# Gated attention on one core: each decay level forms only its own score blocks, ScalarE places the coarse ones, and the fine ones take one masked copy of the diagonal blocks

## The chip, the cores and the metric

The kernel runs on one core of one Trainium2 chip. The metric is the device time of one execution in microseconds (us). The whole of a hybrid encoder block is computed in one launch: an input projection, a gated linear attention and a convolution side by side, an output projection, a cross attention and a mixture of experts. The change lies in the gated linear attention.

## What is computed

Only the attention part is shown. Queries and keys have 64 channels per head, values 128; there are 4 heads, 1024 positions, and a decay per channel and position in each of the two directions.

```python
GLA_HEADS = 4; GLA_DV = 128; GLA_DK = 64; CHUNK = 64
def gla_direction(q, k, v, log_a, strict):
    # o_i = sum_{j<=i (or j<i if strict)} q_i diag(prod_{m=j+1..i} a_m) k_j^T v_j
    bcum = jnp.cumsum(log_a..., axis=-2)
    diff = bcum[..., :, None, :] - bcum[..., None, :, :]
    decay = jnp.exp(jnp.where(mask[:, :, None], diff, -jnp.inf))
    scores = jnp.einsum('bhnid,bhnjd,bhnijd->bhnij', qc, kc, decay)
    o_intra = jnp.einsum('bhnij,bhnjv->bhniv', scores, vc)
    ...
o = rms_norm(o_f + o_b, norm_g)          # forward plus backward direction
return (o * silu(r)).astype(q.dtype)
```

## The kernel before

The instructions of each engine are written out in the order in which they run, one block of code per engine, with semaphores between them; nothing is moved by a scheduler. Only the loop over experts at the end is a hardware loop.

The attention works on windows of 128 positions, 8 of them (`TT`), and on two pairs of heads, `p` = 0 and 1. Within a window the scores of both directions form one 128x128 matrix per head. A product of two decays can't be formed for all pairs of positions from one common reference without overflow, so the matrix is put together from levels. Level 0 is the diagonal (no decay at all). Level l = 1 to 7 takes the pairs of positions whose halves of a block of 2s positions differ, with s = 64, 32, 16, 8, 4, 2, 1 (`LEVELS`): each gets a reference at the middle of its own block. Before the change each level forms the full 128x128 product of every window, and a mask picks the entries that belong to it.

For each `p` the engines run this loop:

- VectorE (DVE), step l: multiplies keys and queries with the decays (`KQ` or `KQ2`, L1242 and L1243, 128x1024 each), computes the exponents of the next level into `EX` (`exponents`, L1209 to L1212, four of 128x512), and then `select(l)`: four instructions that move the products of level l from PSUM into `Ssc`, one bank of four windows each. For l = 0 that is a plain copy (L1225), for the others a copy under a mask (L1227).
- ScalarE (ACT): the exponential of `EX` for each level, one instruction of 128x2048 (L729). After that of level 0 it also drains four products of the memory projection (`drain_memory`, L608).
- TensorE (PE), level l (L1843): 16 matmuls, one per window and head of the pair. Keys of 64 channels are the stationary operand, 128 queries move. Levels alternate between banks 0 to 3 and 4 to 7 of PSUM. The trace shows two matmul records and two weight loads for each of these f32 matmuls, so 32 records a level. Behind level 0 stand two chunks of the memory projection (`memory_chunk`, L1788), 64 records of 256 moving columns, and a wait until ScalarE has drained them, since level 1 takes over their banks.

PE's level l+1 needs DVE's step l (`s_kq`); DVE's `select(l)` needs PE's level l (`s_gram`); PE's level l needs `select(l-2)` to be done with the banks. Behind the loop PE turns the decayed keys (L1855), forms the window updates (L1865), and then the outputs from `Ssc` and the states (L1877 to L1879).

## Time and profile before

| | us |
|---|---|
| median of 3 runs | 2769.03 |
| lowest, highest | 2765.13, 2769.28 |
| the profiled execution | 2766.17 |
| its span in the trace | 2764.4 |
| level loop, p = 0: first KQ to last select | 361.9 to 417.2 |
| level loop, p = 1: memory products 493.1 to 507.1, last select ends | 557.5 |

The profiled execution's own time is 1.8 us longer than the span of its trace. The page gives PE 91% busy, DVE 68%, ScalarE 47%. The expert loop takes the last 1,660 us and most of PE's time; the two level loops take about 55 and 65 us of the span. The granted clock of TensorE has two levels, 2.4 GHz (shown as 1.00) and 1.2 GHz (0.50). A "record" is a line of the trace for one pass of a matmul; its duration holds a latency that overlaps with its neighbours, so prices here are taken from the distance between starts.

### The profile page before, as it was taken

What the parts mean: (1) busy time and instruction counts of PE and PEld (TensorE: products, weight loads), DVE (VectorE), ACT (ScalarE), POOL (GpSimd) and SP (SyncE); (2) the same over time, 40 slices, a digit from 0 to 9 for tenths busy, and PEclk for the clock granted to TensorE, in tenths of its full rate; (3) what the DMA queues carried; (4) which work ended last, traced back from release to release, by engine and by line L of the source; (5) the groups of instructions that cost most, each with busy time, mean ns of one, the idle gap of its engine ahead of it and who ended that gap; (6) DMA issues with size and microseconds to landing.
All of it is one profiled execution on the core that took longest, in us unless ns stands there. A gap on an engine that the chain in (4) does not pass through costs nothing.

```text
span 2764.4 us, 36052 instructions
## 1 busy us (share of the span) xinstructions
PE 2521.2 (91%) x12280; PEld 2064.2 (75%) x12281; DVE 1872.7 (68%) x1955; ACT 1287.3 (47%) x1374; POOL 384.7 (14%) x321
## 2 busy tenths in 40 slices
PE   4999888879897898599999999999999999999994
PEld 3889686859784697477777777777777777777773
DVE  4399693851404325687887787768877778888776
ACT  4211433230314223366665565556555566676554
POOL 0000000001000005211211211122211122121111
PEclk9999865769899995799999999999999999999997
DMA  3111200211010023998997888779878788999776
GB/s 117 51 57 47 76 31 0 77 61 39 31 46 16 1 98 100 312 313 292 340 351 257 274 284 269 256 217 336 280 251 283 261 282 286 339 364 324 245 248 246
DMA packets 268690, 536.19 MB, mean 194 GB/s; under 512 B 11100, under 2 KB 45200, under 8 KB 268528
## 3 DMA queue, kind: packets, MB, share of 16 engines
q1 hardware_dynamic: 249952, 474.51, 48.6%
q0 software_dynamic: 16384, 57.68, 9.0%
q10 hardware_dynamic: 2288, 3.08, 0.4%
q8 instruction: 47, 0.77, 0.1%
q14 instruction: 19, 0.16, 0.0%
HBM read 491.45 MB, written 43.78 MB: 194 GB/s over the span
## 4 chain that ended last, share of the span: by engine, by line
PE 77%; DVE 13%; issue 4%; ACT 4%; DMA 1%; DVEq 1%; ACTq 0%; POOL 0%; POOLq 0%
PE PS L2082 11%; PE PS L2084 11%; PE PS L2083 11%; PE PS L1748 9%; PE PS L2090 6%; PE PS L2087 6%; PE PS L1905 3%; PE PS L1971 3%; DVE wlo L1543 2%; PE PS L2052 1%; PE PS L1958 1%; DVE Ssc L1227 1%; PE PS L1923 1%; PE PS L1925 1%; PE PS L1788 1%
## 5 line engine op out<-in xcount | busy, mean ns | idle before, releaser
L1543 DVE TENSOR_TENSOR wlo<-raw,whi 128x2048 fp32r<-128x2048 f32 x395 | 897.9, 2287 | 202.4 <-ACT whi L864 181.9
L864 ACT CAST whi<-raw 128x2048 fp32r<-128x2048 f32 x395 | 746.0, 1911 | 199.1 <-PE PS L2090 137.6
L2082 PE MATMUL PS<-whi,xhi 128*128 128x512 f32 x1056 | 439.1, 416 | 0.5 <-DVE wlo L1543 0.5
L2084 PE MATMUL PS<-whi,xlo 128*128 128x512 f32 x1056 | 414.0, 392 | 0.0
L2083 PE MATMUL PS<-wlo,xhi 128*128 128x512 f32 x1056 | 412.4, 391 | 0.0
L2084 PEld LDWEIGHTS PS<-whi,xlo 128*128 128x128 f32 x1056 | 198.9, 188 | 43.7
L2082 PEld LDWEIGHTS PS<-whi,xhi 128*128 128x128 f32 x1056 | 200.4, 190 | 39.8 <-DVE wlo L1543 5.2
L2083 PEld LDWEIGHTS PS<-wlo,xhi 128*128 128x128 f32 x1056 | 199.5, 189 | 40.0
L2082 PE MATMUL PS<-whi,hhi 128*128 128x512 f32 x512 | 202.6, 396 | 0.0
L2084 PE MATMUL PS<-whi,hlo 128*128 128x512 f32 x512 | 199.7, 390 | 0.0
L2083 PE MATMUL PS<-wlo,hhi 128*128 128x512 f32 x512 | 199.4, 389 | 0.0
L2090 PE MATMUL PS<-wlo,xtl 128*128 128x512 f32 x480 | 193.5, 403 | 0.0
L2087 PE MATMUL PS<-whi,xtl 128*128 128x512 f32 x480 | 187.5, 391 | 0.0
L507 POOL COPY idxc<-TG 128x2 uint32 (+1 forms) x35 | 23.7, 678 | 917.8 <-PE PS L2052 515.9
L1132 DVE SCALAR_TENSOR_TENSOR yT<-u_pad,CWT,yT 128x1024 f32<-128x1024 f32 x120 | 144.2, 1275 | 0.0
L528 POOL DMA_INDIRECT acc_scratch<-yb,idxs x66 | 135.1, 2047 | 22.0 <-issue 22.0
L513 POOL DMA_INDIRECT xs<-h_scratch,idxc x70 | 132.2, 1889 | 19.9 <-issue 17.7
L920 ACT ACTIVATE yb<-PS,row_gate 128x512 f32<-128x512 f32 x64 | 44.0, 687 | 189.1 <-PE PS L2090 127.0
L1314 DVE TENSOR_TENSOR xres<-xres,PS 128x256 f32<-128x256 f32 x64 | 26.9, 420 | 150.6 <-PE PS L1905 82.0
L2090 PEld LDWEIGHTS PS<-wlo,xtl 128*128 128x128 f32 x480 | 90.0, 188 | 30.4 <-issue 13.6
L2084 PEld LDWEIGHTS PS<-whi,hlo 128*128 128x128 f32 x512 | 96.1, 188 | 20.4
L2082 PEld LDWEIGHTS PS<-whi,hhi 128*128 128x128 f32 x512 | 96.1, 188 | 19.9
(376 smaller groups left out, 4757.7 us busy)
## 6 DMA issues: line engine op xcount, KB each, us to landing
raw<-in_exp_w_up SPq DMA_DIRECT2D x267, 1024.0 KB, 6.1
raw<-in_exp_w_down SPq DMA_DIRECT2D x128, 1024.0 KB, 6.8
ring<-in_w_in SPq DMA_DIRECT2D x11, 1024.0 KB, 5.3
xres<-in_x SPq DMA_DIRECT2D x4, 1024.0 KB, 12.9
ring<-in_xattn_wk SPq DMA_DIRECT2D x4, 1024.0 KB, 6.9
ring<-in_xattn_wv SPq DMA_DIRECT2D x4, 1024.0 KB, 4.9
ring<-in_w_out SPq DMA_DIRECT2D x4, 1024.0 KB, 5.0
xres<-in_x SPq DMA_DIRECT2D x1, 4096.0 KB, 13.4
```

The costliest lines, as they stand in the source:

```text
L513: nc.gpsimd.indirect_dma_start(xs[0:rows, b, :], None, h3_dram, bass.IndirectOffsetOnAxis(ap=idxc[0:rows, b:b + 1], axis=0)).then_inc(s_xs ...
L528: nc.gpsimd.indirect_dma_start(acc_dram, bass.IndirectOffsetOnAxis(ap=idxs[0:rows, b:b + 1], axis=0), yb[0:rows, b, :], None, compute_op=A ...
L864: nc.scalar.copy(whi[:, chunk_slot(c, NSPL), :], raw[chunk_slot(c, NRAW)][:]).then_inc(s_whi, 1)
L1132: ins = nc.vector.scalar_tensor_tensor(out=yT[:, c, :], in0=uc, scalar=w, in1=yT[:, c, :], op0=ALU.mult, op1=ALU.add)
L1543: nc.vector.tensor_tensor(wlo[:, chunk_slot(c, NSPL), :], raw[chunk_slot(c, NRAW)][:], whi[:, chunk_slot(c, NSPL), :].bitcast(F), ALU.subtract
L1748: ins = pe.matmul(out, lhs, rhs, start=(k == 0 and i == 0), stop=(k == KT - 1 and i == 2))
L1905: ins = pe.matmul(bank_groups(n, 256), a, b, start=(k == 0 and i == 0), stop=(k == KT - 1 and i == 2))
L2082: pe.matmul(o, hi[:, k, :], wh, start=first and bias is None, stop=False)
L2083: pe.matmul(o, hi[:, k, :], wl, start=False, stop=False)
L2084: ins = pe.matmul(o, lo[:, k, :], wh, start=False, stop=stop and kk == 3)
L2087: pe.matmul(ot, both_parts, wh, start=first, stop=False)
L2090: ins = pe.matmul(ot, both_parts, wl, start=False, stop=stop and kk == 3)
```

## The change

Level 1 forms only the 64x64 blocks off the diagonal of each window, level 2 only the 32x32 blocks next to the diagonal ones within each half, and level 0 and levels 3 to 7 only the 32x32 blocks on the diagonal. `gram_banks` puts a level into two banks (0 and 1, or 2 and 3), one per head of the pair, so that the memory projection keeps banks 4 to 7 for itself. ScalarE copies level 1 and level 2 into `Ssc` (4 copies each). `select` runs for level 0 and levels 3 to 7 alone, with one instruction over a new tile `Dsc` of 128x512, and at the end ScalarE copies `Dsc` into the diagonal blocks of `Ssc` (4 copies). The exponential is issued in two halves, keys and queries. The last two memory chunks of each `p` are cut into four halves, one behind each of levels 1 to 4. The masks shrink from seven of 128x128 to five of 128x32.

```diff
+        DIAG = (0, 3, 4, 5, 6, 7)
+        def gram_banks(L):
+            return 2 * (L % 2)
+        def diag_scores(L, rows=slice(0, P)):
+            b = gram_banks(L)
+            return PS[rows, b:b + 2, 0:256].rearrange("p h (w c) -> p h w c", w=TT)
...
                 for l in range(8):
-                    act.wait_ge(s_sub, 8 * p + l + 1)
-                    nc.scalar.activation(EX[:], EX[:], ACT.Exp, scale=1.0 / TAU).then_inc(s_ex, 1)
-                    if l == 0:
-                        drain_memory(range(8 * p + 4, 8 * p + 8))
+                    for i in range(2):
+                        act.wait_ge(s_sub, 16 * p + 2 * l + i + 1)
+                        nc.scalar.activation(EX[:, i, :], EX[:, i, :], ACT.Exp, scale=1.0 / TAU).then_inc(s_ex, 1)
+                    if l == 2:
+                        act.wait_ge(s_gram, 2 * (8 * p + 2))
+                        for hh in range(2):
+                            for h in range(2):
+                                rows, cols = slice(64 * h, 64 * (h + 1)), slice(64 * (1 - h), 64 * (2 - h))
+                                ins = nc.scalar.copy(Ssc[rows, hh, :, cols], PS[rows, gram_banks(1) + hh, :].rearrange(
+                                    "p (w c) -> p w c", w=TT))
+                        ins.then_inc(s_plc, 1)
+                    if l == 3:
+                        act.wait_ge(s_gram, 2 * (8 * p + 3))
+                        for q in range(4):
+                            rows, other = slice(32 * q, 32 * (q + 1)), q ^ 1
+                            ins = nc.scalar.copy(scores(rows, slice(32 * other, 32 * (other + 1))), diag_scores(2, rows))
+                        ins.then_inc(s_plc, 1)
+                    if 3 <= l < 7:
+                        drain_memory((8 * p + l + 1,))
...
+                act.wait_ge(s_sel, 6 * (p + 1))
+                for q in range(4):
+                    rows = slice(32 * q, 32 * (q + 1))
+                    ins = nc.scalar.copy(scores(rows, rows), Dsc[rows, :, :, :])
+                ins.then_inc(s_plc, 1)
                 act.wait_ge(s_U, 14 * (p + 1))
...
                 def select(l):
-                    for b in range(4):
-                        hh, half = b // 2, b % 2
-                        L = 8 * p + l
-                        dve.wait_ge(s_gram, 4 * L + b + 1)
...
-                            ins = nc.vector.copy_predicated(
-                                scores, masks[:, l - 1:l, :].broadcast_to([P, 4, P]), products)
-                        ins.then_inc(s_sel, 1)
+                    L = 8 * p + l
+                    dve.wait_ge(s_gram, 2 * (L + 1))
+                    if l == 0:
+                        if p:
+                            dve.wait_ge(s_plc, 3 * p)
+                        ins = nc.vector.tensor_copy(Dsc[:], diag_scores(L))
+                    else:
+                        dve.wait_ge(s_sel, 6 * p + DIAG.index(l))
+                        mask = masks[:, l - 3:l - 2, :].unsqueeze(1).broadcast_to([P, 2, TT, 32])
+                        ins = nc.vector.copy_predicated(Dsc[:], mask, diag_scores(L))
+                    ins.then_inc(s_sel, 1)
...
                         pe.wait_ge(s_kq, 9 * p + l)
-                        if l >= 2:
-                            pe.wait_ge(s_sel, 4 * (L - 1))
+                        if l in (3, 4):
+                            pe.wait_ge(s_plc, 3 * p + l - 2)
+                        elif l >= 2:
+                            pe.wait_ge(s_sel, 6 * p + DIAG.index(l - 2) + 1)
...
+                    size = 64 if l == 1 else 32
+                    for w in range(TT):
+                        for q in range(P // size):
+                            partner = q ^ 1 if l in (1, 2) else q
+                            for hh in range(2):
+                                hp = slice(GDK * hh, GDK * (hh + 1))
+                                keys = slice(P * w + size * q, P * w + size * (q + 1))
+                                queries = slice(P * w + size * partner, P * w + size * (partner + 1))
+                                ins = pe.matmul(PS[size * q:size * (q + 1), gram_banks(L) + hh, size * w:size * (w + 1)],
+                                                K_[hp, keys], Q_[hp, queries], start=True, stop=True)
+                                if w == TT - 1 and q == P // size - 1:
+                                    ins.then_inc(s_gram, 1)
+                    if 1 <= l < 5:
+                        memory_chunk(4 * p + 2 + (l - 1) // 2, ((l - 1) % 2,))
                 pe.wait_ge(s_kq, 9 * p + 8)
-                pe.wait_ge(s_sel, 32 * (p + 1))
+                pe.wait_ge(s_sel, 6 * (p + 1))
```

How the instructions of the loop stand on three engines, for p = 0. PE, before: `x16` is one level of 16 matmuls, `mT,ring` the memory projection (an f32 matmul has two records in the trace), and the row with `ident` is the turning of the keys behind the loop.

```order
L1788 MATMUL PS<-mT,ring 128x256 x32
L1843 MATMUL PS<-qT,kT 128x128 x16
L1788 MATMUL PS<-mT,ring 128x256 x32
L1843 MATMUL PS<-KQ 128x128 x16
L1843 MATMUL PS<-KQ_60 128x128 x16
L1843 MATMUL PS<-KQ 128x128 x16
L1843 MATMUL PS<-KQ_60 128x128 x16
L1843 MATMUL PS<-KQ 128x128 x16
L1843 MATMUL PS<-KQ_60 128x128 x16
L1843 MATMUL PS<-KQ 128x128 x16
L1855 MATMUL PS<-ident,KQ_60 128x128 x16
```

PE, at the same place after the change:

```order
L1822 MATMUL PS<-mT,ring 128x256 x32
L1883 MATMUL PS<-qT,kT 32x32 x64
L1883 MATMUL PS<-KQ 64x64 x32
L1822 MATMUL PS<-mT,ring 128x256 x8
L1883 MATMUL PS<-KQ_60 32x32 x64
L1822 MATMUL PS<-mT,ring 128x256 x8
L1883 MATMUL PS<-KQ 32x32 x64
L1822 MATMUL PS<-mT,ring 128x256 x8
L1883 MATMUL PS<-KQ_60 32x32 x64
L1822 MATMUL PS<-mT,ring 128x256 x8
L1883 MATMUL PS<-KQ 32x32 x64
L1883 MATMUL PS<-KQ_60 32x32 x64
```

The 32 memory matmuls behind level 0 are now four groups of 8 behind levels 1 to 4, and a level has 64 matmuls of 32x32 (32 of 64x64 at level 1) in place of 16.

DVE, before, from the step of level 1 to that of level 3 (the copies into `Ssc` are `select`):

```order
L1242 TENSOR_TENSOR KQ_60<-EX,kT 128x1024
L1243 TENSOR_TENSOR KQ_60<-EX,qT 128x1024
L1209 TENSOR_TENSOR EX<-Bf 128x32x16
L1210 TENSOR_TENSOR EX<-Rb 128x32x16
L1211 TENSOR_TENSOR EX<-Rb 128x32x16
L1212 TENSOR_TENSOR EX<-Bf 128x32x16
L1227 COPY_PREDICATED Ssc<-masks,PS 128x512 x4
L1242 TENSOR_TENSOR KQ<-EX,kT 128x1024
```

DVE after the change, from the exponents that step 3 computes:

```order
L1243 TENSOR_TENSOR EX<-Bf 128x128x4
L1244 TENSOR_TENSOR EX<-Rb 128x128x4
L1245 TENSOR_TENSOR EX<-Rb 128x128x4
L1246 TENSOR_TENSOR EX<-Bf 128x128x4
L1259 COPY_PREDICATED Dsc<-masks,PS 128x512
L1273 TENSOR_TENSOR KQ<-EX,kT 128x1024
```

The four masked copies of a level are one, and steps 1 and 2 have none at all.

ScalarE after the change, from the exponentials of level 0 on (before, this was one exponential of 128x2048, four drains of `kx` and seven more exponentials):

```order
L741 ACTIVATE EX<-EX 128x1024 x6
L747 COPY Ssc<-PS 64x8x64 x4
L741 ACTIVATE EX<-EX 128x1024 x2
L754 COPY Ssc<-PS 32x16x32 x4
L618 COPY kx<-PS 128x256
L741 ACTIVATE EX<-EX 128x1024 x2
L618 COPY kx<-PS 128x256
L741 ACTIVATE EX<-EX 128x1024 x2
L618 COPY kx<-PS 128x256
L741 ACTIVATE EX<-EX 128x1024 x2
L618 COPY kx<-PS 128x256
L741 ACTIVATE EX<-EX 128x1024 x2
```

The placements stand behind the exponentials of levels 2 and 3, and the drains, which stood together behind the first exponential, are spread over levels 3 to 6.

## Rows read from the trace of the kernel before

**Rows 1.** Page, part 4: the chain that ended last, by engine and line

```profile
PE 77%; DVE 13%; issue 4%; ACT 4%; DMA 1%; DVEq 1%; ACTq 0%; POOL 0%; POOLq 0%
```

**Rows 2.** Timeline of one level, p = 0: start us, us, engine, line, names, count, idle before

```profile
388.35 2.55 DVE L1227 COPY_PREDICATED Ssc<-masks,PS 128x512 f32<-128x512 uint8 x4
388.46 1.91 ACT L729 ACTIVATE EX<-EX 128x2048 f32<-128x2048 f32 x1 [5.33 <-DVE EX L1212]
390.80 1.21 DVE L1242 TENSOR_TENSOR KQ<-EX,kT 128x1024 f32<-128x1024 f32 x1
391.92 1.22 DVE L1243 TENSOR_TENSOR KQ<-EX,qT 128x1024 f32<-128x1024 f32 x1
393.17 0.69 DVE L1209 TENSOR_TENSOR EX<-Bf 128x512 f32<-128x512 f32 x1
393.19 6.21 PEld L1843 LDWEIGHTS PS<-KQ 64*128 64x128 f32 x32 [1.03 <-DVE KQ L1243]
393.19 6.50 PE L1843 MATMUL PS<-KQ 64*128 64x128 f32 x32 [0.73 <-DVE KQ L1243]
...
395.59 2.56 DVE L1227 COPY_PREDICATED Ssc<-masks,PS 128x512 f32<-128x512 uint8 x4
```

**Rows 3.** Timeline, p = 0: first step of the loop and its end

```profile
361.88 1.22 DVE L1242 TENSOR_TENSOR KQ<-EX,kT 128x1024 f32<-128x1024 f32 x1
...
364.35 5.87 PEld L1843 LDWEIGHTS PS<-KQ 64*128 64x128 f32 x32 [4.20 <-issue]
...
414.64 2.52 DVE L1227 COPY_PREDICATED Ssc<-masks,PS 128x512 f32<-128x512 uint8 x4
...
417.31 3.65 PE L1855 MATMUL PS<-ident,KQ 128*128 128x128 f32 x16 [3.13 <-DVE Ssc L1227]
418.44 0.58 ACT L735 COPY KEt<-PS 128x512 f32<-128x512 f32 x1 [6.47 <-PE PS L1855]
```

**Rows 4.** Timeline, p = 1: level 0, the memory products, levels 1 and 2, last select

```profile
489.62 3.31 PEld L1843 LDWEIGHTS PS<-qT,kT 64*128 64x128 f32 x32 [0.33 <-issue]
...
491.42 0.21 ACT L725 ACTIVATE TTd<-TTd 128x16 f32<-128x16 f32 x1
491.49 0.68 DVE L1211 TENSOR_TENSOR EX<-Rb 128x512 f32<-128x512 f32 x1
492.09 0.68 DVE L1212 TENSOR_TENSOR EX<-Bf 128x512 f32<-128x512 f32 x1
...
493.05 13.68 PEld L1788 LDWEIGHTS PS<-ring,mT 128*128 128x128 f32 x64
...
507.17 0.37 ACT L608 COPY vx<-PS 128x256 f32<-128x256 f32 x1 [3.08 <-PE PS L1788]
507.44 1.91 ACT L729 ACTIVATE EX<-EX 128x2048 f32<-128x2048 f32 x1
...
507.59 3.30 PEld L1843 LDWEIGHTS PS<-KQ 64*128 64x128 f32 x32 [0.86 <-ACT vx L608]
...
509.38 1.23 DVE L1242 TENSOR_TENSOR KQ<-EX,kT 128x1024 f32<-128x1024 f32 x1 [7.28 <-ACT EX L729]
...
554.96 2.52 DVE L1227 COPY_PREDICATED Ssc<-masks,PS 128x512 f32<-128x512 uint8 x4
```

**Rows 5.** Windows: us, busy of PE, PEld, DVE, ACT, POOL, then the granted clock

```profile
337.00:345.00 8.00, 5.19 (x32) 5.19 (x32) 3.06 (x6) 7.94 (x9) 0.00 (x0) 0.74 0.38 128
345.30:349.00 3.70, 3.70 (x13) 3.08 (x13) 3.67 (x8) 3.67 (x4) 0.00 (x0) 0.68 0.02 4
497.00:507.00 10.00, 10.00 (x47) 8.57 (x46) 5.07 (x9) 0.93 (x3) 0.00 (x0) 1.00 0.30 105
507.60:518.40 10.80, 6.99 (x64) 6.60 (x64) 8.98 (x12) 3.66 (x2) 0.00 (x0) 1.00 0.67 196
518.40:557.00 38.60, 32.53 (x160) 31.05 (x160) 38.43 (x53) 9.55 (x5) 0.00 (x0) 0.50 0.00 0
```

**Rows 6.** L1788 in 345 to 361 us: duration min/median/max ns, first and last start

```profile
L1788 PEld LDWEIGHTS PS<-mT,ring x64: 190/190/337, 345.3 to 360.0; 128*128 128x128 f32 x64
```

**Rows 7.** Timeline, PE: the matmuls with the fewest moving columns

```profile
1035.48 3.46 PE L1984 MATMUL PS<-rw,h3T 128*128 128x32 f32 x16
...
1077.90 0.37 PE L2010 MATMUL PS<-Mb,onesb 128*128 128x32 bf16 x8
...
1237.73 0.71 PE L2056 MATMUL PS<-ident,xs 64*128 64x64 f32 x8
```

**Rows 8.** Groups by line: mean ns, and the idle time of ScalarE before the state products end

```profile
L735 ACT COPY KEt<-PS 128x512 f32<-128x512 f32 x8 | 4.7, 585 | 14.6 <-PE PS L1855 14.6
L608 ACT COPY kx<-PS 128x256 f32<-128x256 f32 x8 | 2.5, 375 | 0.3 <-PE PS L1788 0.3
L737 ACT ACTIVATE EX<-Bf 128x1024 f32<-128x1024 f32 x2 | 2.1, 1056 | 19.7 <-PE PS L1865 19.7
```

**Rows 9.** Timeline of the kernel's start: the last mask, and TensorE's first wait

```profile
6.73 0.29 DVE L1024 SCALAR_TENSOR_TENSOR masks<-xor,mtmp 128x128 uint8<-128x128 int32 x1
7.61 1.06 ACT L589 ACTIVATE sig<-mem_tm 128x1024 f32<-128x1024 f32 x1
```

More of the change, by code:

```diff
@@ L134, in build @@
         before = sb("before", [P, P], F, 198)
-        masks = sb("masks", [P, 7, P], U8, 198.5)
+        masks = sb("masks", [P, 5, 32], U8, 198.5)
         W2 = sb("W2", [2 * RANK, 2, GK], F, 199.5)
@@ L142, in build @@
         smx = sb("smx", [P, 4, 4], F, 203.4375)
-        xor = sb("xor", [P, P], I32, 203.5)
-        mtmp = sb("mtmp", [P, P], F, 204)
+        xor = sb("xor", [P, 32], I32, 203.5)
+        mtmp = sb("mtmp", [P, 32], F, 204)
         PVr = sb("PVr", [64, P], F, 204.5)
@@ L721, in _ @@
                 drain_memory(range(8 * p, 8 * p + 4))
+                scores = lambda rows, cols: Ssc[rows, :, :, cols]
                 if p == 0:
@@ L740, in _ @@
                     act.wait_ge(s_lnv, 19)
+                    act.wait_ge(s_plc, 6)
                     split_y(1)
@@ L1019, in _ @@
             nc.vector.tensor_tensor(xor[:], xor[:], mtmp[:].bitcast(I32), ALU.bitwise_xor).then_inc(s_mask, 1)
-            for l, s in enumerate(LEVELS):
-                dve.wait_ge(s_mask, 2 * l + 1)
+            dve.wait_ge(s_mask, 1)
+            nc.vector.tensor_scalar(xor[:], xor[:], 31, None, ALU.bitwise_and).then_inc(s_mask, 1)
+            for l, s in enumerate(LEVELS[2:]):
+                dve.wait_ge(s_mask, 2 * l + 2)
                 nc.vector.tensor_scalar(mtmp[:], xor[:], float(2 * s), None, ALU.is_lt).then_inc(s_mask, 1)
-                dve.wait_ge(s_mask, 2 * l + 2)
+                dve.wait_ge(s_mask, 2 * l + 3)
                 nc.vector.scalar_tensor_tensor(out=masks[:, l, :], in0=xor[:], scalar=float(s), in1=mtmp[:],
@@ L1112, in _ @@
             w_in_lo(4)
-            dve.wait_ge(s_pad, 2 * CT)
+            dve.wait_ge(s_const, 7 + 2 * CT)
             cv = 0
@@ L1214, in select @@
                 def select(l):
-                    for b in range(4):
-                        hh, half = b // 2, b % 2
-                        L = 8 * p + l
-                        dve.wait_ge(s_gram, 4 * L + b + 1)
-                        if l and b == 0:
-                            dve.wait_ge(s_sel, 4 * L)
-                        scores = Ssc[:, hh, 4 * half:4 * half + 4, :]
-                        products = PS[:, 4 * (L % 2) + b, :].rearrange("p (w c) -> p w c", w=4)
-                        if l == 0:
-                            ins = nc.vector.tensor_copy(scores, products)
-                        else:
-                            ins = nc.vector.copy_predicated(
-                                scores, masks[:, l - 1:l, :].broadcast_to([P, 4, P]), products)
-                        ins.then_inc(s_sel, 1)
+                    L = 8 * p + l
[9 more added lines that the diff above has]
+                    ins.then_inc(s_sel, 1)
                 exponents(0)
@@ L1247, in _ @@
                     else:
-                        nc.vector.tensor_tensor(wins(EX[:, 0, :]), tot(0), wins(Bf[:]), ALU.subtract)
+                        nc.vector.tensor_tensor(wins(EX[:, 0, :]), tot(0), wins(Bf[:]), ALU.subtract
+                                                ).then_inc(s_sub, 1)
                         nc.vector.tensor_tensor(wins(EX[:, 1, :]), tot(1), wins(Rb[:]),
                                                 ALU.subtract).then_inc(s_sub, 1)
-                    select(l)
-                dve.wait_ge(s_ex, 9 * p + 8)
+                    if l in DIAG:
+                        select(l)
+                dve.wait_ge(s_ex, 17 * p + 16)
                 nc.vector.tensor_tensor(KQ2[:, 0, :], EX[:, 0, :], kT[:, p, :], ALU.mult)
@@ L1772, in _, with memory_chunk @@
             norm_turn("x", TT)
-            def memory_chunk(c):
+            def memory_chunk(c, halves=(0, 1)):
                 nonlocal g
                 pe.wait_ge(s_ring[slot_of[g]], 16 * fills[g])
-                for i in range(2):
+                for i in halves:
                     m = 2 * c + i
@@ L1789, in memory_chunk @@
                     ins.then_inc(s_mm["mem"], 1)
-                g += 1
+                if halves[-1] == 1:
+                    g += 1
             n = 0
@@ L1833, in _ @@
                         pe.wait_ge(s_kq, 9 * p + l)
-                        if l >= 2:
-                            pe.wait_ge(s_sel, 4 * (L - 1))
+                        if l in (3, 4):
+                            pe.wait_ge(s_plc, 3 * p + l - 2)
+                        elif l >= 2:
+                            pe.wait_ge(s_sel, 6 * p + DIAG.index(l - 2) + 1)
                     K_, Q_ = (kT[:, p, :], qT[:, p, :]) if l == 0 else (
                         (KQ, KQ2)[(l - 1) % 2][:, i, :] for i in range(2))
-                    for b in range(4):
-                        hh, half = b // 2, b % 2
-                        for w in range(4):
-                            a = slice(P * (4 * half + w), P * (4 * half + w + 1))
-                            hp = slice(GDK * hh, GDK * (hh + 1))
-                            ins = pe.matmul(PS[:, 4 * (L % 2) + b, P * w:P * (w + 1)], K_[hp, a], Q_[hp, a],
-                                            start=True, stop=True)
-                        ins.then_inc(s_gram, 1)
```

26 lines of the change are left out of this document (13 added, 13 removed).

## The prediction

> **What bounds the kernel now.** I read the chain that ended last first: it is PE for 77%, DVE for 13% [rows 1], and most of PE's part is the expert loop, which the change doesn't touch. So the question is what the two level loops cost, and I read them in the timeline, one level at a time. A level of p = 0 repeats every 7.24 us (388.35 to 395.59). DVE never pauses in it: 2.4 us for the two products KQ (390.80 to 393.17), 2.4 us for four exponents, 2.5 us for the four masked copies. PE's 32 records take 6.2 us of it and PE then waits 0.73 us for DVE; ScalarE waits 5.33 us [rows 2]. So DVE sets the loop, but PE is only 0.7 us behind it. In p = 1 something else comes first: 64 records of the memory projection run from 493.05 to 507, ScalarE's drains stand ahead of the exponential, and DVE idles 7.28 us until 509.38 [rows 4]. The ends of the loops are the last select, 414.64 + 2.52 = 417.2 and 554.96 + 2.52 = 557.5, for which the turning of the keys waits [rows 3, 4]. Whatever is saved before these two points shortens the kernel one for one, since all that follows hangs on them.
>
> **DVE's part.** One masked copy of 128x512 costs a quarter of the 2.5 us, 0.62 us: the new select has the same 128x512 elements. So a step falls from 7.24 to 7.24 - 1.85 = 5.4 us, and steps 1 and 2, without a select, to 4.8 us. If nothing else held it, DVE would come out 6 x 1.85 + 2 x 2.47 = 16 us earlier in p = 0, and by more in p = 1, where it waits now. The new form of the instruction reads two banks in place of one; no row shows that, and I take the price per element as unchanged.
>
> **ScalarE's part.** Two exponentials of 128x1024 cost 2 x 1.06 = 2.1 us where one of 128x2048 cost 1.91 [rows 2, 8]; the first half starts while DVE is still at the second, so the result is not later. The placements are 4 copies with 512 elements a partition, at 0.585 us each 2.3 us [rows 8], at levels 2 and 3. With a drain of 0.37 us the fullest step has 2.1 + 2.3 + 0.4 = 4.8 us, below every cycle found here; cover is the 5.33 us that ScalarE idles. Two new waits stand ahead of work on ScalarE: for PE's level 1 and level 2. Behind them are the exponentials of levels 3 and 4, which need DVE's exponents, and these come later than those products in the schedule below. PE's levels 3 and 4 wait for the placements; they too come later by 5 us and more. The last four copies (2.3 us) fall into the 9.9 us in each p in which ScalarE waits for the state products [rows 8]. If that cover were gone they would cost 2.3 us per p. The masks at the start end at 7.0 us, before ScalarE has even begun the first norm's sums [rows 9]: nothing.
>
> **PE's part, on which all hangs.** A level has 128 records of 32 columns in place of 32 records of 128, so as many weight columns as before. What is a short record's price? A record of 128 columns costs (3.30 - 0.19) / 31 = 100 ns at the full clock [rows 4] and (6.21 - 0.33) / 31 = 190 ns at half [rows 2]. The router's matmuls, which move only 32 columns against 128 columns of weights, cost (3.46 - 0.39) / 15 = 205 ns at half clock [rows 7]. So the weight columns set the price, not the moving ones, and a quarter of the columns would be 25 and 48 ns. The shortest spacing in the trace is (0.37 - 0.19) / 7 = 26 ns, at half clock, bf16 with 32 moving columns [rows 7], each with its own weight load; I take no record under 27 ns. Bounds: 27 ns at best, the 190 or 100 ns of today's record at worst. I take 27 ns at the full clock and 48 ns at half, since the same f32 operand, 64 rows high, is nearest. A level then costs 128 x 27 = 3.5 us at the full clock, 6.1 us at half; level 1, 64 records of 64 columns, 3.2 or 6.1 us. One thing could make it cheaper: neighbouring matmuls now alternate between the two halves of the array's rows. The Trainium skill (TensorE: Matmul & The Clock Gate, Part 3) says that matmuls on different row groups run at the same time; no row of this trace has two short ones side by side, and by it the half-clock levels would take 3.5 us and the sum below would gain another 13 us.
>
> A memory half is 16 records. Warm that is 16 x (13.68 - 0.19) / 63 = 3.4 us [rows 4]. From a cold start the 64 records of p = 0 took 14.7 us from first to last start against 13.5, 1.3 us more [rows 6], so 4.7 us.
>
> **The clock.** It stands at 1.00 through the memory products, stays there through two levels (507.6 to 518.4) and is 0.50 for the rest of the loop, though PE is busy 32.5 of 38.6 us in it [rows 5]. It fell within 337 to 345 after a pause and was back within 4 us of the memory products' start. So I take it as 1.00 from level 2 until level 5 (a memory half every 7 us), as 0.50 at levels 6 and 7, and at level 1 as 0.50 in p = 0 (20 us of pause before it) and 1.00 in p = 1.
>
> **The sum.** With these prices PE is the slower one, since its level and a memory half, 6.9 us, exceed DVE's 5.4. p = 0: level 1 starts at 364.3 as now. + 6.1 (level 1) + 4.7 (half) = 375.1; + 3 x (3.5 + 3.4) for levels 2 to 4 = 395.8; + 3.5 (level 5) + 6.1 + 6.1 = 411.5; + 0.8 for the hand-over and the last select = 412.3, against 417.2: -4.9 us. p = 1: the first exponential's query half can follow DVE's exponents (492.8) at 493.9, KQ is done at 495.2, and nothing waits for the memory products any more. 495.2 + 3.2 + 3.4 = 501.8; + 20.7 = 522.5; + 3.5 + 12.2 = 538.2; + 0.8 = 539.0, against 557.5: -18.5 us. Together -23.4 us. The profiled execution took 2766.17 us, so 2742.8; the median of the runs is 2.9 us above that execution, within their own spread of 4 us, so a median could come out at 2743 to 2746. I say 2743.
>
> **Both bounds of the same case.** With 27 ns everywhere DVE sets the second half of the loop: the same working gives 404.0 and 533.7, together -37, 2729. With 40 ns at the full clock levels 2 to 5 take 5.1 us each, -10 us, 2756.
>
> **Rival 1, a short record has a price of its own.** The kernel turns 64-row tiles with 64 moving columns at (0.71 - 0.22) / 7 = 70 ns each at the full clock [rows 7], more than half the price of its double. If 70 ns is what any short f32 record costs, a level is 9.0 us at either clock. p = 0 ends at 440, p = 1 at 571: +36, 2803. It decides from 49 ns on, where both loops sum to what they take now; 60 ns gives +19, 2785. Against it stands the 26 ns row, for it the fact that those are bf16. The Trainium skill (the same page, Part 1) names such a price, about 62 ns for every matmul when the hardware's decoder is off; the 26 ns row says that it is on here, and 62 ns would give 2789. This rival is the slower one; 0.22.
>
> **Rival 2, the clock doesn't hold.** Short matmuls on a quarter of the columns are light work, and 32 records of 128 columns already let the clock fall. If each memory half starts cold (4.7 to 4.9 us) and each level costs 48 ns, the loops end at 427 and 555, together +8, 2774. With the clock low all the way and 6.8 us for each half (16 x 427 ns, twice the warm spacing), +27, 2793. For it: the 0.50 at 518.4 to 557 [rows 5]. Against it: two whole levels without any memory product kept 1.00. 0.12.
>
> **Rival 3, the memory halves eat the gain of p = 0.** They run in PE's idle time now (345 to 360 [rows 6], while DVE prepares the decays) and stand between the levels afterwards. With short records at 45 to 49 ns and a clock that holds, p = 0 loses 5 us and p = 1 gains 5 to 9: 2761 to 2766. 0.08.
>
> **How the numbers follow.** Forecast 0.58 (2729 to 2757), rival 1 0.22 (2772 to 2803 and beyond), rival 2 0.12 (2768 to 2793), rival 3 0.08. The range goes from 2729 to 2793: it leaves out the upper end of rival 1, some 0.11, and 0.04 below. A measurement tells 0.2% from no change, 5.5 us. Faster by more: the forecast, half of rival 3 and a little of the rest, 0.64. Within: the other half of rival 3 and the low end of rival 2, 0.10. Slower: 0.26.
>
> **What would show it.** In the trace of the changed kernel: PE's matmuls of a level, first to last start, 3.5 us at clock 1.00 and 6.1 at 0.50; the granted clock near 1.00 from 376 to 399 and from 489 to 526; memory halves of 3.4 us; one masked copy of 0.7 us a level; DVE idle before it, released by PE, not by ScalarE; the last select at 412 and, counted from the start of level 0 in p = 1 (489.6 before), 49.4 us later. It would be wrong with a spacing over 49 ns, with the clock at 0.50 between the halves, or with DVE waiting for the placements on ScalarE.

## The result, and the profile after

The changed kernel takes 2730.85 us (median of 4 runs, 2719.98 to 2739.17); runs of the kernel before beside it have a median of 2769.16, 38 us more. The ratio on record is 0.9848, 95% interval 0.9829 to 0.9868, which is 42 us of the kernel before (37 to 47). A second timing of the same kernel gave 2731.03 and 0.9864 (0.9848 to 0.9881), 38 us. So the gain is 38 to 42 us, where 2743, 23 us, was forecast. That lies at the fast end of the forecast's range of 2729 to 2793: the median is 2 us inside it, and the ratio, taken of the 2769.03 of before, gives 2727, 2 us outside. The profiled execution took 2719.98 us, its span is 2718.2.

The chain that ended last, as page part 4 gives it for the changed kernel, reads as before [rows 1] but for one point of DVE:

```profile
PE 77%; DVE 12%; issue 4%; ACT 4%; DMA 2%; DVEq 1%; ACTq 0%; POOL 0%; POOLq 0%; SPq 0%
```

One level of p = 0 in the timeline of the changed kernel, the same place as [rows 2]: start us, us, engine, line, names, count, idle before.

```profile
388.15 1.21 DVE L1273 TENSOR_TENSOR KQ<-EX,kT 128x1024 f32<-128x1024 f32 x1
389.28 1.22 DVE L1275 TENSOR_TENSOR KQ<-EX,qT 128x1024 f32<-128x1024 f32 x1
390.53 0.69 DVE L1243 TENSOR_TENSOR EX<-Bf 128x512 f32<-128x512 f32 x1
390.55 1.56 PE L1883 MATMUL PS<-KQ 64*32 64x32 f32 x128 [3.33 <-DVE KQ L1275]
...
391.86 1.06 ACT L741 ACTIVATE EX<-EX 128x1024 f32<-128x1024 f32 x1 [2.89 <-DVE EX L1244]
...
392.94 0.72 DVE L1259 COPY_PREDICATED Dsc<-masks,PS 128x512 f32<-128x512 uint8 x1
...
393.56 1.22 DVE L1273 TENSOR_TENSOR KQ<-EX,kT 128x1024 f32<-128x1024 f32 x1
```

A level takes 393.56 - 388.15 = 5.41 us, where it took 7.24. DVE has no pause in it. PE's 128 short records take 1.56 us in all, 32 records of 128 columns took 6.50, and PE now waits 3.33 us for DVE. PE, which had 0.7 us to spare beside DVE, no longer sets anything here.

The levels behind which a memory half stands, and the ends of the two loops (timeline, changed kernel; the first select is that of p = 0, the second that of p = 1):

```profile
364.56 1.99 PE L1883 MATMUL PS<-KQ 64*64 64x64 f32 x64 [23.14 <-DVE KQ L1275]
366.47 4.70 PE L1822 MATMUL PS<-mT,ring 128*128 128x256 f32 x16
371.10 1.29 PE L1883 MATMUL PS<-KQ 64*32 64x32 f32 x128
372.32 3.72 PE L1822 MATMUL PS<-mT,ring 128*128 128x256 f32 x16
...
401.70 0.71 DVE L1259 COPY_PREDICATED Dsc<-masks,PS 128x512 f32<-128x512 uint8 x1
...
478.17 1.23 DVE L1273 TENSOR_TENSOR KQ<-EX,kT 128x1024 f32<-128x1024 f32 x1 [1.05 <-ACT EX L741]
...
517.73 0.72 DVE L1259 COPY_PREDICATED Dsc<-masks,PS 128x512 f32<-128x512 uint8 x1
```

The loops end at 402.4 and 518.4 us, where they ended at 417.2 and 557.5 [rows 3, 4]: 14.8 us come from p = 0, another 24.3 from p = 1, 39 in all. DVE's wait of 7.28 us in p = 1 [rows 4] is gone, and the first KQ of p = 1, which waited 2.05 us for the exponential before, waits 1.05. The span is 46 us shorter; the other 7 lie behind the loops, where nothing was changed. The stretch from the last output of the attention to the end took between 2151 and 2166 us in the traces of this case (2157 before, 2151 in this one), so the total of a single run can't be read closer than that. The loops are read in the traces, and the sum in several runs.

ScalarE's placements in the same trace: two groups between the exponentials, and one behind the loop, with 6.67 us of idle time after it out of the 9.9 us of before [rows 8]. DVE, which sets the loop, doesn't wait for them, so they cost nothing.

```profile
376.15 2.26 ACT L741 ACTIVATE EX<-EX 128x1024 f32<-128x1024 f32 x2 [0.37 <-DVE EX L1244]
378.43 2.34 ACT L754 COPY Ssc<-PS 32x512 f32<-32x512 f32 x4
...
406.69 2.49 ACT L765 COPY Ssc<-Dsc 32x512 f32<-32x512 f32 x4
...
415.85 1.06 ACT L768 ACTIVATE EX<-Bf 128x1024 f32<-128x1024 f32 x1 [6.67 <-PE PS L1905]
```

### The profile page after: what moved, and what is told of

Read it like the earlier page. It is cut to its first block, busy times and chain, and to the rows that moved or that the text cites. A ratio compares the mean times of both kernels' runs of the same rounds, so it can differ in the third digit from the quotient of the medians.

```text
span 2718.2 us, 38787 instructions
## 1 busy us (share of the span) xinstructions
PE 2442.7 (90%) x13622; PEld 1989.0 (73%) x13689; DVE 1840.1 (68%) x1900; ACT 1303.5 (48%) x1414; POOL 383.1 (14%) x321
## 4 chain that ended last, share of the span: by engine, by line
PE 77%; DVE 12%; issue 4%; ACT 4%; DMA 2%; DVEq 1%; ACTq 0%; POOL 0%; POOLq 0%; SPq 0%
PE PS L2123 12%; PE PS L2125 11%; PE PS L2124 11%; PE PS L1782 9%; PE PS L2131 6%; PE PS L2128 6%; PE PS L1946 3%; PE PS L2012 3%; DVE wlo L1577 1%; PE PS L2093 1%; PE PS L1999 1%; PE PS L1964 1%; PE PS L1966 1%; PE PS L1965 1%; ACT whi L896 1%
## 5 line engine op out<-in xcount | busy, mean ns | idle before, releaser
L2124 PE MATMUL PS<-wlo,xhi 128*128 128x512 f32 x1056 | 412.3, 390 | 0.0
L523 POOL DMA_INDIRECT xs<-h_scratch,idxc x70 | 128.1, 1830 | 20.0 <-issue 17.9
L938 ACT COPY low_up<-PS 64x512 f32<-64x512 f32 x60 | 35.0, 584 | 158.3 <-PE PS L2131 158.3
```

What stands on the lines that cost most here:

```text
L523: nc.gpsimd.indirect_dma_start(xs[0:rows, b, :], None, h3_dram, bass.IndirectOffsetOnAxis(ap=idxc[0:rows, b:b + 1], axis=0)).then_inc(s_xs ...
L2124: pe.matmul(o, hi[:, k, :], wl, start=False, stop=False)
```

## Experiments on the price of a short record

The forecast took 27 to 48 ns for a record; the trace has (1.29 - 0.19) / 127 = 8.7 ns, where 0.19 us is the duration of the last record itself (0.24 us at the lower clock). Neighbouring matmuls of the changed kernel lie on different tiles of the array: heads alternate between row halves, and the four blocks of a window between groups of 32 columns. Theory A is that tiles run side by side and the forecast's price holds for one tile. Theory B is that a short record is cheap by itself.

**same_tile**: consecutive matmuls stay on one tile; only their order differs.

```diff
-                    for w in range(TT):
-                        for q in range(P // size):
-                            partner = q ^ 1 if l in (1, 2) else q
-                            for hh in range(2):
+                    for q in range(P // size):
+                        partner = q ^ 1 if l in (1, 2) else q
+                        for hh in range(2):
+                            for w in range(TT):
```

> The changed kernel with the loops of a level turned round: for each block row and each head the 8 windows follow one another, so that 8 neighbouring matmuls (16 records) use the same 64 rows and the same 32 columns of the array. Theory A (short matmuls of different tiles run side by side, and that makes a record cost 9 ns): without neighbours in other tiles the record goes back to the 25 to 27 ns of the prediction at clock 1.00 and about 50 ns at 0.50; a level takes 3.4 us or 6 us and not 1.3. Theory B (a short weight load is simply cheap, and the tiles have nothing to do with it): 9 ns, a level of 1.3 us, as before the edit. By A the kernel takes 0 to 10 us more than the changed one, by B the same time.

It took 2750.73 us (one run). Timeline of its PE:

```profile
341.57 5.73 PE L1883 MATMUL PS<-qT,kT 64*32 64x32 f32 x128 [4.08 <-DVE EX L1210]
...
381.60 3.72 PE L1822 MATMUL PS<-mT,ring 128*128 128x256 f32 x16
385.25 3.54 PE L1883 MATMUL PS<-KQ 64*32 64x32 f32 x128
388.71 3.72 PE L1822 MATMUL PS<-mT,ring 128*128 128x256 f32 x16
...
412.63 3.65 PE L1895 MATMUL PS<-ident,KQ 128*128 128x128 f32 x16 [1.56 <-DVE KQ L1290]
...
490.49 5.99 PE L1883 MATMUL PS<-KQ 64*64 64x64 f32 x64 [2.04 <-DVE KQ L1275]
...
496.41 5.47 PE L1822 MATMUL PS<-ring,mT 128*128 128x256 f32 x16
501.80 3.54 PE L1883 MATMUL PS<-KQ 64*32 64x32 f32 x128
```

(3.54 - 0.19) / 127 = 26.4 ns a record, the forecast's 27. Level and memory half take 7.1 us, PE has no pause in these levels, and it leads. The granted clock is 0.98 from 376 to 399 us. So theory A holds: what the forecast priced is the record on one tile. At clock 0.50 it is 43 ns there, where 48 was forecast: (5.73 - 0.24) / 127 for the 128 records of level 0, which start at 341.57.

**same_tile_timed**: the same kernel, in rounds.

> The kernel same_tile once more, now timed in rounds beside the kernel before: the changed kernel with its short score matmuls in an order in which neighbours lie on the same tile of the array, all else as it is. Its trace showed a level of 128 short records at 3.54 us and loops that ended where the prediction had put them (412.6 and 543.7 us). By the shift of the loops against the kernel before, 575.0 - 21.7 or so, the difference should be 20 to 24 us, so 2745 to 2749 beside a kernel before of 2769; if what lies behind the loops hangs on how warm TensorE was left, up to 10 us either way.

2750.58 us (2743.4 to 2758.7), ratio 0.991 (0.9876 to 0.9945): 25 us faster than the kernel before (15 to 34). The changed kernel wasn't in these rounds. Against its own rounds same_tile is 20 us slower by the medians, 13 to 17 us by the ratios, and its two loops end 22 us later in the traces. The order of the matmuls alone decides about half of the gain: 22 of the 39 us in the loops.

**two_row_halves** (heads alternate, one column group after another) and **column_tiles** (one head after the other, the four column groups in turn):

```diff
+                    for q in range(P // size):
+                        partner = q ^ 1 if l in (1, 2) else q
+                        for w in range(TT):
+                            for hh in range(2):
```

```diff
+                    for hh in range(2):
+                        for w in range(TT):
+                            for q in range(P // size):
+                                partner = q ^ 1 if l in (1, 2) else q
```

> The changed kernel with the block row outermost, then windows, then heads: neighbours alternate between the two halves of the array's rows but stay in the same 32 columns. Theory A (each of the 8 tiles works by itself): 2 tiles side by side, 12 to 14 ns a record at clock 1.00 and up to 25 at 0.50, a level of 1.6 to 3.4 us. Theory B: 9 ns, 1.3 us.

> The changed kernel with the head outermost, then windows, then block rows: neighbours go round the four column tiles within one half of the rows. Theory A: 4 tiles side by side, 7 to 13 ns a record, a level of 1.0 to 1.7 us. Theory B: 9 ns. If only the row halves matter and the columns do not, 25 ns and 3.4 us.

2727.32 and 2735.11 us (one run each). PE of two_row_halves, then of column_tiles, timelines:

```profile
371.16 1.94 PE L1883 MATMUL PS<-KQ 64*32 64x32 f32 x128
```

```profile
365.15 3.32 PE L1883 MATMUL PS<-KQ 64*64 64x64 f32 x64 [23.04 <-DVE KQ L1275]
...
388.69 1.32 PE L1883 MATMUL PS<-KQ 64*32 64x32 f32 x128
```

Two row halves: (1.94 - 0.19) / 127 = 13.8 ns, half of 26.4. Four column groups within one row half: 1.32 us, 8.9 ns, a third and not a quarter. Both at once, the changed kernel, 8.7 ns. At the full clock eight tiles give no more than four: at 8.7 ns something else sets the pace, and what it is wasn't found. The last levels of the changed kernel, at clock 0.50, still have (1.56 - 0.24) / 127 = 10.4 ns where the forecast took 48; there column_tiles has 12.8. Both orders are fast enough for DVE to lead nearly throughout, so their loops end within 0.8 us of the changed kernel's, and what their totals differ by is not in the loops. One rival stays open for two_row_halves and for before_alt below: heads that alternate also alternate between two banks of PSUM. In column_tiles neighbours stay in one bank and are fast all the same.

**before_alt**: the kernel before, its 16 matmuls of 64x128 a level with heads alternating.

> The kernel before, with its full 128x128 products, but with the heads of the pair alternating from matmul to matmul, so that neighbours use the two halves of the array's rows; VectorE's select waits for the whole level. Theory A: two tiles side by side halve the price of a record, from 100 and 190 ns to about 50 and 95, and a level from 6.2 us to about 3.2 us at clock 0.50. Theory B: 190 ns and 6.2 us as before. The kernel's time stays within 5 us of the one before by both, since VectorE sets that loop.

2767.15 us (one run); the one run of the kernel before beside it took 2776.19, and its runs in the other groups 2765 to 2778, so no gain can be told. The level loops end where they did or later (418.8 and 557.8 us against 417.2 and 557.5). PE by groups from 366 to 417 us: names, count, busy us, mean ns, idle time before; first the kernel before, then before_alt, and one level from the timeline of before_alt.

```profile
L1843 PE MATMUL PS<-KQ 64*128 64x128 f32 x217 | 43.9, 427 | 4.6 <-DVE KQ L1243 4.6
```

```profile
L1844 PE MATMUL PS<-KQ 64*128 64x128 f32 x224 | 25.5, 415 | 25.5 <-DVE KQ L1243 25.5
```

```profile
402.08 3.78 PE L1844 MATMUL PS<-KQ 64*128 64x128 f32 x32 [3.45 <-DVE KQ L1243]
```

Records of 128 moving columns get cheaper by alternating heads too: PE is busy 25.5 us of the stretch instead of 43.9, and what it saves turns into waiting for DVE. The mean clock differs a little (0.61 against 0.50), but a level that runs at 0.50 in both, at 402.08 in before_alt, takes 3.78 us instead of 6.50 [rows 2]. Cheap scores alone were worth nothing in the old loop; they pay only where DVE is made shorter as well.

## Experiments on what leads now

**again**: the changed kernel once more, as the reference of this group. **select_x4**: three more copies of the score banks, 128x512 each, ahead of each select.

```diff
+                    for i in range(3):
+                        n = 18 * p + 3 * DIAG.index(l) + i
+                        dve.wait_ge(s_dx, TAPS * CT + n)
+                        nc.vector.tensor_copy(Dx[:], diag_scores(L)).then_inc(s_dx, 1)
                     if l == 0:
```

> The changed kernel once more, for its spread and a second trace: 2720 to 2740 us, some 35 to 45 us under the one before. If the spread of 19 us between its runs comes from the level loops, their ends move between the two traces; if it comes from behind them, the level loops agree within 1 us and a later stage differs.

> The changed kernel with three extra copies of 128x512 from the same banks into a spare tile ahead of each of the 12 selects, so that VectorE pays four such instructions again at these steps. If VectorE sets the loops, each extra copy costs its 0.6 us: 12 x 3 x 0.6 = 22 us slower than the changed kernel. If TensorE or ScalarE set them, less than 8 us.

The loops of again end at 403.0 and 519.1 us, 0.6 and 0.7 us after those of the first trace, and its span is 7.2 us longer: 6.5 us of the spread lie behind the loops.

2731.03 and 2751.65 us (ratio 0.9931, 0.9914 to 0.9948): 20.6 us for what DVE was given. The last select of p = 1 ends at 541.7 us, with again at 519.1: 22.6.

```profile
384.33 2.13 DVE L1257 COPY Dx<-PS 128x512 f32<-128x512 f32 x3
386.38 0.72 DVE L1265 COPY_PREDICATED Dsc<-masks,PS 128x512 f32<-128x512 uint8 x1
386.99 1.20 DVE L1279 TENSOR_TENSOR KQ<-EX,kT 128x1024 f32<-128x1024 f32 x1
```

These rows (timeline of select_x4) have no gap: six selects of 2.05 us more in each of two loops make 24.6, and nearly all of it comes out at the end. DVE sets both loops.

**one_exp**: the exponential in one instruction again, behind all four exponents.

```diff
-                    for i in range(2):
-                        act.wait_ge(s_sub, 16 * p + 2 * l + i + 1)
-                        nc.scalar.activation(EX[:, i, :], EX[:, i, :], ACT.Exp, scale=1.0 / TAU).then_inc(s_ex, 1)
+                    act.wait_ge(s_sub, 16 * p + 2 * l + 2)
+                    nc.scalar.activation(EX[:], EX[:], ACT.Exp, scale=1.0 / TAU).then_inc(s_ex, 2)
```

> The changed kernel with one exponential over keys and queries in place of two halves. By the schedule of the trace a step is then bound by exponents (ready 4.8 us after the step's start), hand-over 0.1, exponential 1.9: 6.8 us in place of 5.4 and 4.8, so 1.4 us more in five steps and 2 us more in two, 10 to 12 us in each p, 20 to 24 us in all. Rival: the halves are worth nothing since ScalarE idles 3 us a step, under 3 us.

2754.8 us, ratio 0.9947 (0.993 to 0.9963): 24 us slower than again, loops' end 542.9, 23.8 later. Timeline of one_exp:

```profile
374.42 1.91 ACT L740 ACTIVATE EX<-EX 128x2048 f32<-128x2048 f32 x1 [5.01 <-DVE EX L1245]
...
376.37 1.22 DVE L1272 TENSOR_TENSOR KQ<-EX,kT 128x1024 f32<-128x1024 f32 x1 [2.04 <-ACT EX L740]
```

In the kernel before, DVE's 2.5 us of masked copies ran while ScalarE formed the exponential [rows 2]. With them gone DVE waits 2.04 us for it at a level without a select. The edit that looked like a detail is worth more than half of the gain, as long as the others are in place.

**mem_back**: the memory products again as one block of 64 records behind level 0, with the wait for their drains, and the drains again behind the first exponential.

```diff
-                    if 1 <= l < 5:
-                        memory_chunk(4 * p + 2 + (l - 1) // 2, ((l - 1) % 2,))
+                    if l == 0:
+                        memory_chunk(4 * p + 2)
+                        memory_chunk(4 * p + 3)
+                        pe.wait_ge(s_dr["mem"], 8 * (p + 1))
```

> The changed kernel with the last two memory chunks of each p behind level 0 again, undivided, with their drains behind the first exponential and PE's wait for them. The interleaving's own share: in p = 1 the exponential of level 1 waits for the drains again, 7 to 12 us later; in p = 0 nothing. 7 to 14 us slower than the changed kernel. Rival (the whole gain of p = 1 above that of p = 0 has another source): 0 to 3 us.

2734.78 us, ratio 0.9876 (0.986 to 0.9893), 3.8 us above again by the medians; its loops end 7.7 us later (526.75), 1.0 of that in p = 0. In the loops that is the low end of what was expected. In the time it is a miss: 3.8 us lie between the 7 to 14 that were expected and the rival's 0 to 3, and the intervals of the two ratios overlap. Timeline of mem_back, p = 1:

```profile
490.54 0.37 ACT L618 COPY vx<-PS 128x256 f32<-128x256 f32 x1 [3.08 <-PE PS L1822]
490.81 2.00 ACT L741 ACTIVATE EX<-EX 128x1024 f32<-128x1024 f32 x2
...
491.90 1.22 DVE L1273 TENSOR_TENSOR KQ<-EX,kT 128x1024 f32<-128x1024 f32 x1 [7.69 <-ACT EX L741]
```

The wait of [rows 4] is back, 7.69 us: the exponential stands behind the drains. In the two traces the stretch behind the loops is 2.8 us shorter in mem_back, which would make up for part of it; why the medians show only 4 of the 7.7 us wasn't settled.

## A kernel that uses it further

The outputs and states behind the loop use 64-row tiles too, one after another. **outputs_grouped** forms four output blocks at a time: four score matmuls, then eight products with the state, heads alternating. The outputs go over eight banks of PSUM instead of four.

```diff
-                    pe.matmul(o, Ssc[:, hh, w, :], v_tm[:, w, P * h:P * (h + 1)], start=True, stop=False)
-                    pe.matmul(o, KQ[hp, 0, tw], ST[hp, 0, w, :], start=False, stop=False)
-                    pe.matmul(o, KQ[hp, 1, tw], ST[hp, 1, w, :], start=False, stop=True).then_inc(s_op, 1)
...
+                    for i in range(i0, i0 + 4):
...
+                        pe.matmul(PS[:, i % 8, 0:P], Ssc[:, hh, w, :], v_tm[:, w, P * h:P * (h + 1)],
+                                  start=True, stop=False)
+                    for d in range(2):
+                        for i in range(i0, i0 + 4):
...
+                            ins = pe.matmul(PS[:, i % 8, 0:P], KQ[hp, d, tw], ST[hp, d, w, :], start=False, stop=d == 1)
```

> Edit, in the changed kernel's output stage: the three matmuls of each 128-row output block are no longer in a row; four blocks' score matmuls come first, then the four blocks' products with the state, which lie on 64 partitions each, heads in turn, so that neighbours use different row halves; outputs go over eight PSUM banks instead of four. Nothing is left out. In the trace of the changed kernel one block costs TensorE 1.8 to 1.9 us (three matmuls of 0.42 to 0.50 us and the changes between them), ScalarE 0.73 us (0.28 + 0.19 + 0.26), at a granted clock of 0.50. Theory A (records on different 64-row halves overlap, as the score blocks on different tiles do): four score matmuls 4 x 0.42, eight half-height ones at 4 x 0.42 to 0.5, so 3.4 to 3.7 us for four blocks, 0.85 to 0.95 a block, ScalarE close behind; the stage falls from some 30 to some 15 us in each of two passes, total 25 to 32 us faster than the changed kernel, some 2700. Theory B (matmuls of 128 columns are long enough that only their own streaming counts, and halves don't overlap): 1.25 to 1.4 us a block, 7 to 10 us a pass, some 2713 to 2717. If the cost of a block lies neither in the row halves nor in the changes between them, no difference.

2690.72 us (2690.17 to 2692.47), ratio 0.9701 (0.9679 to 0.9723): 40 us below the changed kernel by the medians, 45 by the ratios of two different rounds, and by either more than expected. Timelines, first the changed kernel (two outputs), then outputs_grouped (eight):

```profile
424.21 0.79 PE L1918 MATMUL PS<-v_tm,Ssc 128*128 128x128 f32 x2
424.94 0.79 PE L1919 MATMUL PS<-ST,KQ 64*128 64x128 f32 x2
425.52 0.63 PE L1920 MATMUL PS<-ST,KQ 64*128 64x128 f32 x2
426.09 0.79 PE L1918 MATMUL PS<-v_tm,Ssc 128*128 128x128 f32 x2
```

```profile
519.83 1.82 PE L1923 MATMUL PS<-ST,KQ 64*128 64x128 f32 x16
...
521.58 1.16 PE L1916 MATMUL PS<-v_tm,Ssc 128*128 128x128 f32 x8
522.67 1.16 PE L1923 MATMUL PS<-ST,KQ 64*128 64x128 f32 x16
523.76 1.16 PE L1916 MATMUL PS<-v_tm,Ssc 128*128 128x128 f32 x8
```

One output cost 426.09 - 424.21 = 1.88 us; four cost 523.76 - 521.58 = 2.18, 0.55 each. The stage fell from 29.9 to 11.6 us in p = 0 (450.3 - 420.5 against 434.2 - 422.6), to 10.4 in p = 1. Two things are mixed in it: the order, and the clock, which was 0.50 throughout the old stage (window 545 to 570) and is 0.89 from 515 to 530 here. The first group of p = 0 runs at 0.50 from 422.6 to 426.6 and tells them apart (timeline of outputs_grouped):

```profile
422.59 2.08 PE L1916 MATMUL PS<-v_tm,Ssc 128*128 128x128 f32 x8 [4.65 <-DVE KQ L1313]
424.60 2.08 PE L1923 MATMUL PS<-ST,KQ 64*128 64x128 f32 x16
426.61 2.07 PE L1916 MATMUL PS<-v_tm,Ssc 128*128 128x128 f32 x8
...
523.64 0.28 ACT L779 ACTIVATE sig<-PS 128x128 f32<-128x128 f32 x1 [0.37 <-PE PS L1923]
```

Four outputs take 426.61 - 422.59 = 4.02 us there, 1.0 each: at the same clock the order takes an output from 1.88 to 1.0 us, and the clock takes it on to 0.55. In 2.01 us pass 8 full-height records or 16 half-height ones, though both change banks from matmul to matmul; so a change of bank by itself doesn't overlap them. How much of the 0.88 us is the overlap of row halves and how much the fewer changes between full and half height was not told apart, nor was the step from four to eight banks. ScalarE still waits 0.37 us for PE in every group of four (last row), so PE leads here too.

**states_and_outputs** adds to it that the update of a window is formed by two matmuls of 64x128 results in the two halves of the partitions, so that DVE advances both heads in one operation.

```diff
-                    pe.matmul(PS[:, 4 + i % 4, 0:256], KEt[:, m // 4, P * (m % 4):P * (m % 4 + 1)],
-                              v_tm[:, w, 256 * p:256 * (p + 1)], start=True, stop=True).then_inc(s_U, 1)
+                    for hh in range(2):
+                        ins = pe.matmul(PS[GDK * hh:GDK * (hh + 1), 4 + i % 4, 0:P],
+                                        KEt[:, m // 4, P * (m % 4) + GDK * hh:P * (m % 4) + GDK * (hh + 1)],
+                                        v_tm[:, w, 256 * p + P * hh:256 * p + P * (hh + 1)], start=True, stop=True)
+                    ins.then_inc(s_U, 1)
...
-                    for hh in range(2):
...
+                    nc.vector.scalar_tensor_tensor(
+                        out=ST[:, d, to, :], in0=ST[:, d, w, :], scalar=TTd[:, 1, d, w:w + 1],
+                        in1=PS[:, 4 + n % 4, 0:P], op0=ALU.mult, op1=ALU.add).then_inc(s_st, 1)
```

> The kernel outputs_grouped with one more edit, in the stage of the states: the update of a window, k^T v of two heads, is formed as two matmuls of 64 columns of weights by 128 columns of data, one in each half of the PSUM partitions and both in the same 128 columns, in place of one matmul of 128 by 256 of which half was thrown away; VectorE then advances both heads' states by one operation of 128x128 in place of two of 64x128. Nothing is left out. The trace of the changed kernel has 28 to 30 pairs of VectorE operations of 0.35 us in a pass, 0.74 us a pair, one pair after another. Theory: the one operation costs what one of the pair did, 0.35 to 0.40 us, and the two matmuls, on different column halves, overlap and stay under it; 14 windows by two halves by 0.35 = 4 to 5 us in the stretch where VectorE leads, up to 9 us a pass if all of the pairs were on the path; total 8 to 18 us below outputs_grouped. Rival: the update is then bound by the round from TensorE to VectorE, 0.5 us and more, and 0 to 5 us come of it.

2677.67 us (2677.16 to 2681.23), ratio 0.9656 (0.9633 to 0.9679): 13 us below outputs_grouped, 53 below the changed kernel, and the fastest of all. Groups of the states' update, first outputs_grouped (402 to 424 us), then this kernel:

```profile
409.83 10.32 DVE L1306 SCALAR_TENSOR_TENSOR ST<-ST,TTd,PS 64x128 f32<-64x128 f32 x28 [5.01 <-PE PS L1905]
```

```profile
407.10 3.71 DVE L1304 SCALAR_TENSOR_TENSOR ST<-ST,TTd,PS 128x128 f32<-128x128 f32 x14 [4.73 <-PE PS L1903]
```

28 operations of 0.35 us in pairs are 14 of the same duration, one behind another: 3.7 us for 10.3. From the turning of the keys to the outputs 12.6 us pass instead of 17.9.

## Why the prediction was wrong

**The step that failed** is the price of a short record, "I take no record under 27 ns". It was mis-sized by three: 8.7 ns. The rows it was taken from [rows 2, 4, 7] are right for what they show, records behind one another on one tile; same_tile measured 26.4 ns. The change sends neighbours to eight tiles. The text saw that row halves alternate and quoted the rule that they run at the same time (the Trainium skill, TensorE: Matmul & The Clock Gate, Part 3), but it worked the rule out for the half-clock levels alone (13 us), kept 27 ns as the floor of any record, and gave no chance to anything below. It overlooked the column groups, which the diff shows in the output's partitions, `PS[size * q:size * (q + 1), ...]`. The runs agree with that rule: 26.4 ns on one tile, 13.8 over two row halves. The same section of the Trainium skill has a weight load overlap only with work on another row group; column_tiles, with one row half at a time, reached 8.9 ns, so here that limit did not bind.

**What followed from it.** With PE at 8.7 ns DVE leads from the first level, and the forecast's own figures for DVE fit: 5.4 and 4.8 us a step (5.41 and 4.81 to 4.88 measured), 16 us earlier in p = 0 (14.8). Its lower bound, 27 ns everywhere, gave 37 us because DVE led in part of it; the loops gave 39.

**A second step that was costed at nothing:** the exponential's halves, "so the result is not later". That is true against the end of one long exponential, and hidden where PE leads. Where DVE leads they are worth 24 us (one_exp). The cover was the masked copies that the same change removes, and the prediction didn't ask what DVE would wait for without them.

**The sum on its own terms.** same_tile comes nearest to the kernel that the forecast described, and its agreement in p = 0 is in part luck. Its loop ends at 412.5 us, forecast 412.3. But level 2 starts at 378.13 and not at 375.1: level 1 began 1.8 us late, and the first memory half took 6.2 us and not 4.7. Levels 6 and 7, put at 0.50 and 6.1 us each, ran at the higher clock (0.97 from 399 to 412 us) at some 26 ns a record, which gave back what had been lost. In p = 1 the forecast puts the end at 539.0, less the 4.9 of p = 0: 534.1; measured 540.4. Of the 6.3 us, 4.7 lie in level 1 and its memory half, taken as warm (3.2 and 3.4 us) but measured at 490.49 and 496.41 as 5.9 and 5.4 between starts: after 2 us of pause PE ran there at the lower clock (0.50 from 490 to 499). So the price of 27 ns and the sum of a level and a half hold, and which stretches run at which clock was not forecast well. The total of that kernel is 25 us below the kernel before, and the forecast's 23 is in its interval.

**The rest.** Memory halves: 3.65 us between starts warm and 4.63 cold, forecast 3.4 and 4.7. Clock of the changed kernel: not 1.00 but 0.78 from 376 to 399 us. It stands at 0.50 in the levels at 390.55 and 395.96, each behind a pause of PE of over 3 us; it cost nothing, since these levels still leave PE over 3 us to spare. Masked copy 0.72 us, as put. Placements cost nothing, as put, but not for the reason given: PE's levels 3 and 4 were to come "later by 5 us and more" than the placements they wait for. With PE this early the placement of level 2 ends at 378.43 + 2.34 = 380.77 and PE's level 4 starts at 380.92, so nearly all of that margin is gone, and in a kernel in which PE leads it would have shown. The last select came at 402.4, not 412, and DVE did not idle before it. In p = 1 KQ was done 5.4 us after level 0's start (480.5 after 475.1), forecast 5.6. Rivals 1 to 3 all made the record or the halves dearer; none occurred. The error lay on the side for which no rival was written.

## What to carry to other kernels

Before a matmul is priced from a row of the trace, write down on which rows of the array its weights and on which partitions its output lie, and those of its neighbours: a price from a sequence on one tile was three times too high here for records of 32 columns that lie on eight. When a step of an engine is removed, ask what ran under its cover; here a 1.9 us exponential had to be cut in two for the gain to arrive. And where small matmuls on half of the array wait in turn with full ones, group them: the same arithmetic in another order, over eight banks instead of four, took 40 us off this kernel.

## What the hardware showed that I had not expected

- A record of 32 weight columns and 32 moving columns in f32: 26.4 ns start to start on one tile, 13.8 over two row halves, 8.9 over four column groups, 8.7 over eight tiles. At clock 0.50 it is 43 on one tile, 12.8 over four column groups, (1.86 - 0.24) / 127, and 10.4 over eight tiles.
- Records of 64 by 64 over the four tiles of a window and two heads: (1.57 - 0.31) / 63 = 20 ns where the clock was 0.72 on average, (1.99 - 0.31) / 63 = 27 ns at 0.50 (the last record lasts 0.31 us). On one tile, in same_tile, (5.99 - 0.31) / 63 = 90 ns at 0.50.
- In p = 1 of the changed kernel PE stops within a level for 0.6 to 1.5 us with "issue" as the reason, and waits for nothing that the profile shows:

```profile
506.58 0.86 PE L1883 MATMUL PS<-KQ 64*32 64x32 f32 x76 [2.11 <-DVE KQ L1275]
508.96 0.79 PE L1883 MATMUL PS<-KQ 64*32 64x32 f32 x52 [1.53 <-issue]
```

The page counts 58 packets of the instruction queue, 0.95 MB, 47 and 0.77 MB before, and the two loops have 704 more matmuls; that PE waited for its instructions is argued, not shown. It cost nothing in the changed kernel, where DVE led. In same_tile one such pause, at 531.91, is 3.3 us long.
